# All depthwise-convolution taps of the mixer on the vector engine, the last ten beside the gated half of the output projection, and the LayerNorm sums later in that half

## The reference

```python
z = h @ w_in                                                  # 1024 -> 2560
glu = z[..., :512] * sigmoid(z[..., 512:1024])
a = causal_dwconv(glu, st_a, wa) + ba                         # width 31, 512 channels
an = (a - mean(a)) * rsqrt(var(a) + LN_EPS) * lg + lb         # over the 512 channels
a_out = an * sigmoid(an)
b_out = gate_b * causal_dwconv(gate_c * x_t, st_b, wb)        # width 3, 512 channels
y = concatenate([a_out, b_out]) @ w_out                       # 1024 -> 1024
```

## Time and profile before

| | us |
|---|---|
| time, median of 3 runs (2745.17 to 2745.77) | 2745.41 |
| the profiled execution's own time | 2743.18 |
| its span (first to last instruction) | 2741.4 |
| PE busy (96% of the span) | 2634.0 |
| DVE busy (52%) | 1435.6 |
| POOL busy (29%) | 782.2 |
| ACT busy (23%) | 627.5 |

### The profile page before, as it was taken

How to read it: one execution, slowest core, us unless ns; L and a number is a source line. 1 busy time by engine, 2 the same in 40 slices (tenths; PEclk the granted TensorE clock), 3 DMA queues, 4 the chain that set the end, 5 groups by cost and what they waited for, 6 DMA issues and landing times.

```text
span 2741.4 us, 41727 instructions
## 1 busy us (share of the span) xinstructions
PE 2634.0 (96%) x17498; PEld 2465.1 (90%) x17498; DVE 1435.6 (52%) x1985; ACT 627.5 (23%) x930; POOL 782.2 (29%) x432
## 2 busy tenths in 40 slices
PE   6999699999999999999999999979999999999996
PEld 6988699999999999997777777759999999999995
DVE  6899856444444444456555555561544444444445
ACT  4110133111111111133333333342311111111111
POOL 5323325332233333340011011023433333233332
PEclk9999899999999999999999999999999999999997
DMA  6433294444444444643443444423111111111111
GB/s 198 161 131 123 92 180 167 164 168 169 169 169 169 169 168 164 219 159 123 143 167 127 166 153 155 148 91 135 47 47 47 42 44 47 47 47 47 47 42 64
DMA packets 93863, 336.70 MB, mean 123 GB/s; under 512 B 22528, under 2 KB 39808, under 8 KB 91136
## 3 DMA queue, kind: packets, MB, share of 16 engines
q1 hardware_dynamic: 93696, 334.20, 36.6%
HBM read 315.88 MB, written 152.25 MB: 171 GB/s over the span
## 4 chain that ended last, share of the span: by engine, by line
PE 87%; DVE 9%; issue 1%; ACT 1%; POOL 1%; DMA 0%; POOLq 0%; DVEq 0%; SPq 0%; ACTq 0%
PE reg L620 44%; PE reg L656 19%; PE reg L847 9%; DVE g L1458 4%; PE reg L725 3%; PE reg L827 3%; PE ob L883 2%; PE reg L868 1%; PE reg L800 1%; DVE neg_s L1685 1%; PE ob L868 1%; PE reg L936 1%; PE reg L638 1%; PE reg L923 1%; PE ob L699 1%
## 5 line engine op out<-in xcount | busy, mean ns | idle before, releaser
L620 PE MATMUL reg<-xs,w_sp 128*128 128x352 f32 x8208 | 1347.1, 326 | 33.8 <-DVE xs L1424 20.8
L620 PEld LDWEIGHTS reg<-xs,w_sp 128*128 128x128 f32 x8208 | 1335.3, 189 | 41.7 <-issue 30.3
L382 POOL TENSOR_TENSOR w_sp<-w_raw,w_sp 128x1024 fp32r<-128x1024 f32 x172 | 426.5, 2480 | 1068.2 <-ACT w_sp L377 1066.5
L656 PE MATMUL reg<-hid,w_sp 128*128 128x352 f32 x3168 | 514.3, 324 | 0.0
L656 PEld LDWEIGHTS reg<-hid,w_sp 128*128 128x128 f32 x3168 | 511.5, 188 | 0.0
L377 ACT ACTIVATE w_sp<-w_raw 128x1024 fp32r<-128x1024 f32 x172 | 182.3, 1060 | 1138.4 <-PE reg L620 713.1
L1435 DVE TENSOR_TENSOR h<-reg,h 128x1056 f32<-128x1056 f32 x200 | 251.4, 1257 | 305.0 <-PE reg L656 235.0
L847 PE MATMUL reg<-xs,w_sp 128*128 128x352 f32 x1512 | 279.6, 332 | 0.0
L1591 DVE TENSOR_TENSOR g<-reg,rst 128x1056 f32<-128x1056 f32 x44 | 55.4, 1259 | 414.7 <-PE reg L620 414.7
L847 PEld LDWEIGHTS reg<-xs,w_sp 128*128 128x128 f32 x1512 | 240.6, 189 | 17.7 <-issue 17.6
L400 POOL TENSOR_TENSOR w_sp<-w_raw,w_sp 128x1024 fp32r<-128x1024 f32 x21 | 49.9, 2375 | 479.9 <-ACT w_sp L395 461.1
(11 more groups left out here) (178 smaller groups left out, 1978.5 us busy)
## 6 DMA issues: line engine op xcount, KB each, us to landing
w_raw<-in_wstream SPq DMA_DIRECT2D x193, 512.0 KB, 3.6
out_sk<-in_cache_k SPq DMA_DIRECT2D x16, 4088.0 KB, 15.4
out_sv<-in_cache_v SPq DMA_DIRECT2D x16, 4088.0 KB, 15.3
kvr<-in_kva SPq DMA_DIRECT2D x16, 2048.0 KB, 9.3
kvr<-in_kvb SPq DMA_DIRECT2D x16, 1536.0 KB, 6.9
wt<-in_wtab SPq DMA_DIRECT2D x16, 512.0 KB, 5.1
h<-in_xT SPq DMA_DIRECT2D x4, 1056.0 KB, 10.0
h_spill<-h SPq DMA_DIRECT2D x8, 528.0 KB, 2.6
```

The source lines that it names most:

```text
L382: nc.gpsimd.tensor_tensor(w_sp[:, u % 3, 1, :], w_raw[:, u % 3, :], w_sp[:, u % 3, 0, :].bitcast(F32), ALU.subtract).then_inc(w_lo, 1)
L620: mm = nc.tensor.matmul(out[:, t, :], w[:, wh, k * P:(k + 1) * P], xs[:, xh, k, t * TS:(t + 1) * TS], start=(n == 0 and wh + xh == 0), sto ...
L656: mm = nc.tensor.matmul(out[:, t, :], w[:, wh, kk * 512 + m * P:kk * 512 + (m + 1) * P], hid[:, par_g, kk, xh, t * TS:(t + 1) * TS], start ...
```

## The change

- `conv_part`, the diagonal matrices and the `cv_init` copies are gone. `TAPS` now holds 4 x 31 = 124 entries, all for DVE. The first tap of each chunk is a `tensor_scalar` (product plus bias), as it was for chunk 0 alone.
- 19 x 6 = 114 of them stand behind units 1 to 19. The last ten stand behind the four `rest_lo` of the B half, with the adds of B0 and B1 between them, and the `acc` addition behind.
- `MEAN_USE` moves from B0 to B4 and `VAR_USE` from B4 to B6. ACT copies the four high parts before it waits for the sample mean, and now splits three weight units, not two, between its squares and the root.

```diff
-MEAN_USE, VAR_USE = B_USE[0], B_USE[4]
+MEAN_USE, VAR_USE = B_USE[4], B_USE[6]
...
-PE_TAPS = 6
-TAPS = [(0, k) for k in range(KA)] + [(c, k) for c in range(1, CA) for k in range(PE_TAPS, KA)]
+TAPS = [(c, k) for c in range(CA) for k in range(KA)]
 PER = 6
-DONE_AT = [max(n for n, (c, _) in enumerate(TAPS) if c == c0) // PER + 1 for c0 in range(CA)]
-CONV_BEHIND = {5: 1, 8: 2, 12: 3}
-DIAG_BEHIND = {3: 1, 6: 2, 10: 3}
...
             for u in range(2, 20):
                 in_proj(u, FIRST[u])
-                if u in CONV_BEHIND:
-                    conv_part(CONV_BEHIND[u])
...
             for u in range(8, 20):
                 hi_after(act, u)
-                behind(u)
-
-            act.wait_ge(ln_full, 1)
-            nc.scalar.activation(mean_s[:, :], ob[:, 0, 0:NS], ACT.Copy).then_inc(ln_std, 1)
             act.wait_ge(full, LAST[19] + 1)
             for c in range(CA):
                 act.wait_ge(free, FIRST[10 + 3 * c] + 1)
                 nc.scalar.activation(xs[:, 0, c, :], cb[:, c, :], ACT.Copy).then_inc(x_hi, 1)
 
+            act.wait_ge(ln_full, 1)
+            nc.scalar.activation(mean_s[:, :], ob[:, 0, 0:NS], ACT.Copy).then_inc(ln_std, 1)
...
-                if k == (PE_TAPS if c else 0):
+                if k == 0:
                     conv_sample(c)
-                    if c:
-                        dve.wait_ge(cv_init, c)
-                if k == 0:
                     chain(nc.vector.tensor_scalar(y, src, w, pc("ba", c), ALU.mult, ALU.add))
...
-            assert len(TAPS) <= PER * 19
-
-
-
             for c in range(CA):
                 rest_lo(1, c, c, cb[:, c, :])
+            for n, (tc, tk) in enumerate(TAPS[PER * 19:]):
+                if n == 4:
+                    add_to_h(B_USE[0], 0)
+                if n == 8:
+                    add_to_h(B_USE[1], 1)
+                conv_tap(tc, tk)
+            add_to_h(B_USE[2], 2)
+            add_to_h(B_USE[3], 3)
             dve.wait_ge(ln_std, 1)
...
-            for m in range(4):
-                add_to_h(B_USE[m], m)
+            add_to_h(B_USE[4], 4)
+            add_to_h(B_USE[5], 5)
             dve.wait_ge(ln_std, 2)
             chain(nc.vector.reciprocal(tmp[:, NP_:], tmp[:, NP_:]))
             dve.wait_ge(std_ok, 3)
             chain(nc.vector.reciprocal(tmp[:, 0:NP_], tmp[:, 0:NP_]))
-            add_to_h(B_USE[4], 4)
             dve.wait_ge(ycen_ok, 2 * CA)
             for c in range(CA):
                 nc.vector.tensor_tensor(Y[c], Y[c], tmp[:, :], ALU.mult).then_inc(yn_ok, 1)
-            add_to_h(B_USE[5], 5)
             rest_lo(1, CA, CA, Y[0])
             rest_lo(1, CA + 1, CA + 1, Y[1])
             add_to_h(B_USE[6], 6)
```

More of the change, by code:

```diff
@@ L238, in build @@
         cb, o2 = place("cb", [P, CA, T], F32, o2)
-        diag, o2 = place("diag", [P, PE_TAPS, P], F32, o2)
         assert o2 <= M0 + 2 * 2 * 2 * T * 4
@@ L314, in build @@
         pads_ok = sem("pads_ok")
-        diag_ok, cv_full, cv_init, cv_done = (sem(s) for s in ("diag_ok", "cv_full", "cv_init", "cv_done"))
+        cv_done = sem("cv_done")
         sigr_ok, cr_ok, cb_ok, cbr_ok = (sem(s) for s in ("sigr_ok", "cr_ok", "cb_ok", "cbr_ok"))
@@ L1046, in _ @@
             std_parts(2)
[L1047 to L1062, removed]
             for c in range(CA):
@@ L1067, in _ @@
                     hi_after(act, 2 * c)
-                    behind(2 * c)
                 act.wait_ge(free, FIRST[2 * c] + 1)
@@ L1073, in _ @@
                 hi_after(act, 2 * c + 1)
-                behind(2 * c + 1)
             for u in range(8, 20):
                 hi_after(act, u)
-                behind(u)
-            act.wait_ge(ln_full, 1)
-            nc.scalar.activation(mean_s[:, :], ob[:, 0, 0:NS], ACT.Copy).then_inc(ln_std, 1)
             act.wait_ge(full, LAST[19] + 1)
```

## The result

The changed kernel takes 2762.23 us (median of 4 runs, 2758.15 to 2763.21) against 2745.29 us for the kernel before (2744.86 to 2745.77): a ratio of 1.0059, 95% interval 1.0041 to 1.0076. I had forecast 2750.1 and a range up to 2757. The profiled execution has a span of 2759.6 us, 18.2 more than before.

What follows compares the result with a forecast made beforehand. PE was taken to bound the kernel over the span, DVE the mixer from 167.15 to 319.36 us. Terms -8.0, +0.4, +3.8, +0.1, +6.1 and +2.3 gave +4.7 on 2745.41: 2750.1 us, range 2744 to 2757.

Steps and rivals of the forecast that it cites:

- 1. Start of B0: Mixer up to the B half: DVE's idle stretches vanish, B0 starts at 314.9 instead of 322.81, 8.0 us gained.
- Charging collisions per POOL operation: Taps on DVE: POOL's work is unchanged, so no extra collision time; charging per tap would give +9 us.
- 2. B0 to B6: First B half uses: late taps cost nothing, but PE waits 3.8 us at B6 for unit 23's split; low clock +0.4.
- 3. B6 to A0: Second sums to the A half: a 16.3 us chain starts A0 at 379.4, PE waiting about 6 us.
- 4. Behind A0: From A0 on: low clock after the wait costs 2.3 us, bounds 0 and 3.5.
- More collisions: Rival before B0: two to four more taps meet POOL, 2 us each, about 2755 us; chance 18%.
- a clock that stays low in the projection: Rival from unit 10 on: PE becomes the bound, up to 8 us a unit, +80 over ten; chance 5%.
- The clock did not hold at A0: Denies the rival that A0's 6 us wait ends before the clock is low for long: 2747.8 us, chance 15%.

Runs made afterwards that it cites:

- sp_unit27: Changed kernel with weight unit 27's load moved ahead of the ten state stores and the first FFN state load: 2747.66 us, ratio 1.0013 to the kernel before.
- before_split_late: Kernel before with ACT making the high parts of units 23 and 24 behind the variance's root, not ahead: 2763.94 us, ratio 1.0067.
- both_fixes: Changed kernel with unit 23's split ahead of the squares, sums at B3 and B5, unit 27's load ahead of the stores: 2738.88 us, 0.9979 of the kernel before.
- before_unit27: Kernel before with only unit 27's load moved ahead of the state stores: 2745.55 us, ratio 1.0002.

## Why the prediction was wrong, by its own steps

*1. Start of B0: right.* The G step was forecast at 304.4 and stands at 304.51, B0 at 314.9 and 315.13. The steps of units 6 and 9, and DVE around the G step, in the changed kernel:

```profile
113.01 1.26 DVE L1443 TENSOR_TENSOR tmp<-reg,rst 128x1056 f32<-128x1056 f32 x1
...
155.16 1.26 DVE L1458 TENSOR_TENSOR sil<-reg,tmp 128x1056 f32<-128x1056 f32 x1
...
304.51 1.26 DVE L1479 TENSOR_TENSOR cb<-reg,cb 128x1056 f32<-128x1056 f32 x1
305.81 7.89 DVE L1414 SCALAR_TENSOR_TENSOR g<-g,pt,g 128x1024 f32<-128x1024 f32 x6
313.73 4.77 DVE L1390 TENSOR_TENSOR xs<-cb,xs 128x1056 fp32r<-128x1056 f32 x4
318.41 5.24 DVE L1414 SCALAR_TENSOR_TENSOR g<-g,pt,g 128x1024 f32<-128x1024 f32 x4
```

Units 6 and 9 no longer keep DVE waiting. Unit 6's step starts 1.3 us later than reckoned (113.01 for 111.7) and the stretch from there takes 1.2 us less (191.5 for 192.7), so part of the hit is luck. The six taps and the four behind them run at 1.31 us each, with no collision, since POOL is idle from 299.4 to 347.3. Charging collisions per POOL operation was the right choice: the 82 taps of the group that answers to the earlier trace rows have a mean of 1.752 us, 36 us in all above 1.315, for 38 before. Some collisions moved to another step: the four `prod` products of `conv_sample` take 2.15 us each for 1.19, 3.8 us in all. So the sum is 40 for 38 us.

*2. B0 to B6: right.* `acc` was ready at 335.2 (forecast 335.3); first sums at 340.12 (forecast 340.7); B6 at 357.62 (358.3) behind a wait of 3.76 us (3.8), released by POOL's split.

*3. B6 to A0: right in its chain, with the clock under-sized.* Wait 6.18 us (about 6), A0 at 380.21 (379.4). From the sums' end, 360.85 + 2.99 = 363.84, to A0 it is 16.4 us (16.3). The stretch from B6's start to that end took 6.2 us for 4.8, because the clock fell to 0.50 at 358 to 362 and the first nine matmuls took 2.99 us and the sums 2.99. The forecast let 1.1 us of lost clock fall there; it was 2.5. That B6 began 0.7 us early hides half of it.

*4. Behind A0: this step failed.* It charged the clock, 2.3 us (measured 1.7). But it rested on the sentence ahead of step 1 that behind A0 "the order on every engine is the old one, PE is the bound, and a shift of A0 reaches the end undiminished". The order of each engine's instructions was the old one, its times were not. Step 2 had found the split of unit 23 late and priced only PE's wait for it. A weight slot has a second waiter, SP, and behind SP's wait stand a cache copy, ten stores, a state load and unit 27. The missing term is 13.1 us in the trace; by `sp_unit27`, whose ratio is 1.0013 for 1.0059, it is 12.6 us (0.0046 x 2745; the two intervals allow some 5 us either way). `before_split_late` shows it with neither half of the change present. Of the queues that the moved split touches the forecast followed PE's, DVE's, ACT's and POOL's, and not SP's.

*Rivals.* More collisions, and a clock that stays low in the projection, did not come: the windows there show a granted clock of 0.66 to 0.83 in the worst stretches of 10 us up to 290 us, and from unit 6 to the G step DVE never waited for PE. The clock did not hold at A0 either: it was at 0.50 at 378 to 382. The outcome lies above the range for a reason that none of the rivals held.

The rows agree with a figure of the Trainium skill, DMA: Bandwidth & Descriptors (Specifications), by which a transfer below 512 bytes does not reach the line rate. Windows of the changed kernel during the stores and, last, with cache copy and weights:

```profile
374.00:378.00 4.00, 0.03 (x1) 0.00 (x0) 3.94 (x5) 3.94 (x5) 0.00 (x0) 0.84 1.80 29
378.00:382.00 4.00, 1.79 (x6) 1.82 (x7) 3.27 (x3) 3.94 (x4) 0.00 (x0) 0.50 1.67 19
...
406.00:410.00 4.00, 0.00 (x0) 0.00 (x0) 1.83 (x2) 2.14 (x3) 2.35 (x1) 0.50 1.44 585
```

The last three columns are the granted clock, the DMA engines' busy share, which counts overlapping packets, and GB/s; of 9926 packets between 300 and 430 us 8768 are under 512 bytes. Small stores keep the engines as busy at 19 to 29 GB/s as large transfers do at 585. Whether unit 27's 11.5 to 12 us come from these stores, from the state load or from the two units issued right behind it, no run separates.

## What to carry to other kernels

When an edit makes a buffer free later, list everyone who waits for it, the transfer queue among them, and follow that queue to the next load that somebody needs: an in-order queue with slow stores in it turned a delay of 15 us in a split that PE missed by 3.8 us into 11.4 us somewhere else. Look at the margin of that load too: here it was 0.2 us, since the transfer took 11.5 us behind the stores where it takes 3.5 by itself. Put the load that is needed soonest ahead of stores that nobody waits for. And a chain that is to hide under a fixed stretch of work should be placed by its length: 16.3 us fit under 21.9, not under 10.2. What decides is how much of the covering engine's work is left behind the point where the chain starts.

## What the runs showed of the hardware that I had not expected

An issue on SP's queue can hold it far longer than its size says: the stores `out_sB`, 8 KB each, have issues of 0.72 to 8.85 us (median 5.7) in the changed kernel, with 14 to 20 us from issue to landing. The first `out_sB` has 8.50 us in the kernel before and 8.85 in the changed one, where the cache copy was issued 2.5 us ahead and took some 16 us. In `both_fixes`, where the copy was issued 15 us ahead, the first two have 0.58 and 0.62 us, and all ten stores take 19 us of the queue for 30. That points at the copy; it was not tried by itself, and it does not explain why a later store takes 0.7 and the next 5.8.

The same 512 KB load of a weight unit landed in 3.4 to 3.9 us with nothing right ahead of it, in 8.8 to 13.2 behind the stores and the state load, and in 16.8 right behind a 4 MB cache copy (`sp_unit27`, 1.65 us behind its issue). With the copy issued 10.8 us ahead it took 10.9 us (`before_unit27`), with 12.9 us ahead 3.9 (`both_fixes`).
